# LayerNorm sums of a two-layer decoder step: the last tile is added on VectorE and the totals go to TensorE as high and low fp32r parts

## The reference, cut to what matters

```python
D_MODEL, D_FF, DEPTH, SEQ, DEC_BATCH, DEC_SEQ = 1024, 2816, 2, 256, 8, 4

def _layernorm(x, g, b):
    mu = jnp.mean(xf, axis=-1, keepdims=True)
    var = jnp.mean(jnp.square(xf - mu), axis=-1, keepdims=True)
    y = (xf - mu) * lax.rsqrt(var + LN_EPS) * g + b

def _layer(x, k_mem, v_mem, conv_buf, lru_buf, h0, W):
    x = _layernorm(DN_ALPHA * x + 0.5 * _swiglu(x, ffn1_wg, ffn1_wu, ffn1_wd), ln1_g, ln1_b)
    m, new_conv, new_lru_buf, h_last = _mixer(x, ...)
    x = _layernorm(DN_ALPHA * x + m, ln2_g, ln2_b)
    x = _layernorm(DN_ALPHA * x + 0.5 * _swiglu(x, ffn2_wg, ffn2_wu, ffn2_wd), ln3_g, ln3_b)
    return x, new_conv, new_lru_buf, h_last
```

## Time and profile before

| | us |
|---|---|
| median of 3 runs | 1402.26 |
| lowest and highest run | 1397.68 and 1403.48 |
| the profiled execution, its own time | 1398.62 |
| the profiled execution, its span | 1396.7 |

### The profile page before, as it was taken

How to read it: one execution, slowest core, us unless ns; L and a number is a source line. 1 busy time by engine, 2 the same in 40 slices (tenths; PEclk the granted TensorE clock), 3 DMA queues, 4 the chain that set the end, 5 groups by cost and what they waited for, 6 DMA issues and landing times.

```text
span 1396.7 us, 25445 instructions
## 1 busy us (share of the span) xinstructions
PE 1376.4 (99%) x10566; PEld 1357.0 (97%) x10566; DVE 898.2 (64%) x1180; ACT 666.4 (48%) x896; POOL 35.1 (3%) x68
## 2 busy tenths in 40 slices
PE   8999999999999999999999999999999999999996
PEld 8999999999899999999999999999998999999996
DVE  5555568586865885554685555686887568655444
ACT  5444446445444664444474444463544456544433
POOL 0100000000110000000000000000001000000000
PEclk9999999999999999999999999999999999999998
DMA  6644444654746454444445544445465453554441
GB/s 237 206 178 158 151 168 157 232 176 159 257 176 207 164 182 157 174 155 162 167 166 179 180 155 149 168 164 197 166 236 199 158 195 134 181 178 154 172 166 57
DMA packets 39997, 243.60 MB, mean 174 GB/s; under 512 B 4576, under 2 KB 4592, under 8 KB 16368
## 3 DMA queue, kind: packets, MB, share of 16 engines
q1 hardware_dynamic: 33264, 219.00, 44.9%
q0 software_dynamic: 5936, 22.01, 4.4%
q10 hardware_dynamic: 720, 1.47, 0.3%
HBM read 238.97 MB, written 3.50 MB: 174 GB/s over the span
## 4 chain that ended last, share of the span: by engine, by line
PE 92%; DVE 4%; DMA 1%; ACT 1%; issue 1%; DVEq 0%; ACTq 0%
PE ps L438 29%; PE ps L437 29%; PE ps L439 29%; DVE wlo L1021 1%; DMA raw<-in_w_in 1%; PE ps L525 1%; PE ps L629 1%; PE ps L652 0%; PE ps L597 0%; ACT whi L725 0%; PE ps L636 0%; DMA raw<-in_ffn_wg 0%; PE ps L469 0%; PE ps L470 0%; PE ps L474 0%
## 5 line engine op out<-in xcount | busy, mean ns | idle before, releaser
L1021 DVE TENSOR_TENSOR wlo<-raw,whi 128x1024 fp32r<-128x1024 f32 (+1 forms) x450 | 511.2, 1142 | 320.1 <-ACT whi L725 315.6
L725 ACT CAST whi<-raw 128x1024 fp32r<-128x1024 f32 (+1 forms) x446 | 437.9, 987 | 507.7 <-PE ps L439 394.7
L437 PE MATMUL ps<-xh,whi 128*128 128x288 f32 (+1 forms) x2144 | 635.1, 296 | 1.6 <-DVE xl L1220 1.1
L438 PE MATMUL ps<-xl,whi 128*128 128x288 f32 (+1 forms) x2144 | 631.3, 294 | 0.0
L439 PE MATMUL ps<-xh,wlo 128*128 128x288 f32 (+1 forms) x2144 | 630.6, 294 | 0.0
L437 PEld LDWEIGHTS ps<-xh,whi 128*128 128x128 f32 x2144 | 404.6, 189 | 3.6 <-DVE xl L1220 1.6
L438 PEld LDWEIGHTS ps<-xl,whi 128*128 128x128 f32 x2144 | 406.5, 190 | 0.8
L439 PEld LDWEIGHTS ps<-xh,wlo 128*128 128x128 f32 x2144 | 405.6, 189 | 0.0
L437 PE MATMUL ps<-hh,whi 128*128 128x288 f32 (+1 forms) x1088 | 322.2, 296 | 0.0
L439 PE MATMUL ps<-hh,wlo 128*128 128x288 f32 (+1 forms) x1088 | 319.4, 294 | 0.0
L438 PE MATMUL ps<-hl,whi 128*128 128x288 f32 (+1 forms) x1088 | 319.4, 294 | 0.0
(11 more groups left out here) (186 smaller groups left out, 745.7 us busy)
## 6 DMA issues: line engine op xcount, KB each, us to landing
raw<-in_w_in SPq DMA_DIRECT2D x48, 1024.0 KB, 4.9
raw<-in_ffn_wg SPq DMA_DIRECT2D x43, 1024.0 KB, 4.8
raw<-in_ffn_wu SPq DMA_DIRECT2D x43, 1024.0 KB, 4.8
raw<-in_ffn_wd SPq DMA_DIRECT2D x32, 1024.0 KB, 4.9
raw<-in_ffn_wd SPq DMA_DIRECT2D x16, 768.0 KB, 4.2
pool<-in_cache_k POOLq DMA_DIRECT2D x16, 512.0 KB, 4.3
pool<-in_cache_v POOLq DMA_DIRECT2D x16, 512.0 KB, 4.5
raw<-in_w_o SPq DMA_DIRECT2D x8, 1024.0 KB, 5.0
```

Of the source, the lines that this page charges most:

```text
L437: mm(out, wh, mh, start=start, stop=False)
L438: mm(out, wh, ml, start=False, stop=False)
L725: s_.copy(whi[:, s, k0:k1, :], raw[:, s, k0:k1, :]).then_inc(hi_ready, 1)
L1021: return v.tensor_tensor(out, full, high.bitcast(F32), sub)
```

## The change

For norms 0 to 4 the two early float32 matmuls of `sums` are left out of `last_block`, and so are the two of the eighth tile. VectorE adds the eighth tile and its square to `sums` as well (two additions of 128x288). ScalarE casts both totals to fp32r high parts, into the tiles `hh[20]` and `hh[21]` that the stage no longer needs, and VectorE makes the low parts in `hl[20]` and `hl[21]`. Four fp32r matmuls, `stat_parts(0)` behind the second tile of the early block and `stat_parts(1)` behind its third, multiply them with `ones`. Norm 5 keeps the old form. The sums are the same in number and position; two semaphores `stat_hi` and `stat_lo` are new, and `summed` now counts ten steps for each norm.

```diff
--- before.py
+++ after.py
@@ -148,7 +148,8 @@
         kt = sb("kt", [P, AH, M])
         vt = sb("vt", [P, MT, AH * HEAD])
         ident = sb("ident", [P, P])
-        ones = sb("ones", [P, P])
+        ones_r = sb("ones", [P, P], F32R)
+        ones = ones_r[:, :].bitcast(F32)
         bd = sb("bd", [P, 2, KB, P])
         pts = sb("pts", [P, L, NPR])
         sts = sb("sts", [P, L, KB, NST])
@@ -248,6 +249,7 @@
         ffn_tanh, ffn_hi, h_ready = sem("ffn_tanh"), sem("ffn_hi"), sem("h_ready")
 
         summed, sq_ready, stats_psum = sem("summed"), sem("sq_ready"), sem("stats_psum")
+        stat_hi, stat_lo = sem("stat_hi"), sem("stat_lo")
         mean_ready, msq_ready, var_ready, rstd_ready = sem("mean_ready"), sem("msq_ready"), sem("var_ready"), sem("rstd_ready")
         centred, normed, y_last = sem("centred"), sem("normed"), sem("y_last")
         fill_out = sem("fill_out")
@@ -381,7 +383,7 @@
             pool_e.wait_ge(consts, 1)
             g.affine_select(out=ident[:, :], in_=ident[:, :], compare_op=ALU.not_equal, fill=1.0, base=0,
                             pattern=[[-1, P]], channel_multiplier=1).then_inc(consts, 1)
-            g.memset(ones[:, :], 1.0 / D).then_inc(consts, 1)
+            g.memset(ones, 1.0 / D).then_inc(consts, 1)
             for i, c in enumerate((4.0, 2.0, 4.0)):
                 g.memset(eps[:, i:i + 1], EPS * c * c).then_inc(consts, 1)
             g.memset(junk[:, :], 1.0).then_inc(consts, 1)
@@ -476,7 +478,7 @@
                     if k in (KD // 2 - 1, KD - 1):
                         last.then_inc(pe_half, 1)
 
-            def early_block(n, q, blocks, behind_first):
+            def early_block(n, q, blocks, behind):
 
                 s = n % 2
                 pe.wait_ge(drained, n - blocks)
@@ -488,8 +490,8 @@
                             c = slice(t * P, (t + 1) * P)
                             last = products(ps[:, t, 0:T + 2], whi[:, s, k, c], wlo[:, s, k, c],
                                             xh_wide[:, k, 0:T + 2], xl_wide[:, k, 0:T + 2], k == 0, k == KD - 1)
-                        if k == 0:
-                            behind_first()
+                        if k in behind:
+                            behind[k]()
                     last.then_inc(pe_half, 1)
 
             def first_of_x(n, q):
@@ -522,16 +524,23 @@
                 q, s, fills = 3 * l + ln, n % 2, gap(3 * l + ln)
 
                 def stat(kind, tile, first=False, last=False):
-                    return mm(ps[:, 4 + kind, 0:T], ones[:, :], tile, start=first, stop=last)
+                    return mm(ps[:, 4 + kind, 0:T], ones, tile, start=first, stop=last)
+
+                def stat_parts(kind):
+                    pe.wait_ge(stat_hi, 2 * q + kind + 1)
+                    pe.wait_ge(stat_lo, 2 * q + kind + 1)
+                    mm(ps[:, 4 + kind, 0:T], ones_r[:, :], hh[:, KF - 2 + kind, :], start=True, stop=False)
+                    mm(ps[:, 4 + kind, 0:T], ones_r[:, :], hl[:, KF - 2 + kind, :],
+                       start=False, stop=True).then_inc(stats_psum, 1)
 
                 cut = halves(K)[0][1]
                 for t in range(2):
                     for k in range(K):
                         if t == 0 and k in (0, cut):
                             pe.wait_ge(lo_ready, 2 * n + (k > 0) + 1)
-                        if t == 1 and k == K - 1:
+                        if t == 1 and k == K - 1 and q == 3 * L - 1:
                             for kind in range(2):
-                                pe.wait_ge(summed, 8 * q + 7 + kind)
+                                pe.wait_ge(summed, 10 * q + 7 + kind)
                                 stat(kind, sums[:, kind, 0, :], first=True)
                         mh, ml = operand(k)
                         c = slice(t * P, (t + 1) * P)
@@ -551,7 +560,7 @@
                 if q == 3 * L - 1:
                     stats()
                     return
-                early_block(n + 1, q, blocks, stats)
+                early_block(n + 1, q, blocks, {1: lambda: stat_parts(0), 2: lambda: stat_parts(1)})
                 if fills:
                     pe.wait_ge(mem_lo, 2 * (splits.index(q) + 1))
                     fill(*fills[0])
@@ -836,6 +845,9 @@
                     act.wait_ge(drained, n + 1)
                     s_.activation(sq[:, 1, :], y[:, KD - 1, :], ACT.Square).then_inc(sq_ready, 1)
                     if more:
+                        for kind in range(2):
+                            act.wait_ge(summed, 10 * q + 9 + kind)
+                            s_.copy(hh[:, KF - 2 + kind, :], sums[:, kind, 0, :]).then_inc(stat_hi, 1)
                         gained(l, ln, KD - 1)
                     act.wait_ge(stats_psum, 2 * q + 1)
                     s_.activation(msq[:, :], ps[:, 4, 0:T], ACT.Square).then_inc(msq_ready, 1)
@@ -1138,7 +1150,7 @@
                                            ps[:, bank:bank + 2, 0:T], mult, add).then_inc(drained, blocks)
 
                 def sum_pair(n, j, q):
-                    done, squared = 8 * q, 5 * q
+                    done, squared = 10 * q, 5 * q
                     if j == 0:
                         return
                     dve.wait_ge(drained, n + 1)
@@ -1181,7 +1193,7 @@
                             dve.wait_ge(y_tail, q + 1)
                         else:
                             dve.wait_ge(sq_ready, 5 * q + 4)
-                        dve.wait_ge(summed, 8 * q + 5 + kind)
+                        dve.wait_ge(summed, 10 * q + 5 + kind)
                         v.tensor_tensor(sums[:, kind, 0], sums[:, kind, 0], tile, add).then_inc(summed, 1)
                     if ln == 1:
                         gained_pair(PAIRS_D - 2, l, ln)
@@ -1193,8 +1205,17 @@
                     v.scalar_tensor_tensor(y[:, KD - 1, :], x[:, KD - 1, :], scale, ps[:, bank + 1, 0:T],
                                            mult, add).then_inc(drained, blocks)
                     if more:
+                        for kind, tile in enumerate((y[:, KD - 1, :], sq[:, 1, :])):
+                            if kind == 0:
+                                dve.wait_ge(drained, n + 1)
+                            else:
+                                dve.wait_ge(sq_ready, 5 * q + 5)
+                            dve.wait_ge(summed, 10 * q + 7 + kind)
+                            v.tensor_tensor(sums[:, kind, 0], sums[:, kind, 0], tile, add).then_inc(summed, 1)
+                        for kind in range(2):
+                            dve.wait_ge(stat_hi, 2 * q + kind + 1)
+                            rest(hl[:, KF - 2 + kind, :], sums[:, kind, 0, :], hh[:, KF - 2 + kind, :]).then_inc(stat_lo, 1)
                         lo(n + 2, 0)
-                        dve.wait_ge(drained, n + 1)
                         gained(l, ln, KD - 1)
                     dve.wait_ge(stats_psum, 2 * q + 2)
                     dve.wait_ge(msq_ready, q + 1)
```

## The result

| | before | after |
|---|---|---|
| median of 10 runs, us | 1402.02 | 1408.31 |
| lowest and highest, us | 1397.08 and 1406.68 | 1402.94 and 1410.64 |
| ratio to before, 95% interval | | 1.0039 (1.0024 to 1.0054) |
| the profiled execution's own time, us | 1398.62 | 1402.94 |
| its span, us | 1396.7 | 1401.0 |

What follows compares the result with a forecast made beforehand. The prediction took TensorE's matmul stream, busy 99%, and waits opening in it at the norms as the bound. It summed 3 x 0.37 + 1.35 + 2.0 = +4.5 us onto 1402.3, giving 1406.8 us, range 1399 to 1412.

Steps and rivals of the forecast that it cites:

- The shift of the chain: VectorE's work behind the eighth tile, variance and tiles of x included, moves 2.0 us later; bounds 1.5 and 2.4.
- The early block at norms 0, 2, 3: TensorE waits 0.64 plus 0.11 us before the first new matmuls and leaves the block 0.75 us ahead of before.
- Behind it: After the early block at norms 0, 2, 3, a later half split makes TensorE 0.37 us later at the fifth tile.
- The margin of 0.77: Slack in us between the second half split of the first block on x and TensorE's fifth tile, after hand-over.
- Tile eight at norms 1 and 4 is held by VectorE: Tile eight comes no earlier there; TensorE waits 1.90 plus 0.11 us, leaving norm 1's early block 0.2 us later.
- Norm 1, +1.35: Behind norm 1's early block the split comes 2.0 us later, so 1.35 us are lost at the fifth tile.
- a rival at 6%: Clock falls to half rate behind new waits at norms 1 and 4: 6.4 us more, +10.9 in all, 1413.2; 6%.
- the sign that I had named for a loss of over 7 us: A granted clock under 1 behind norms 1 or 4 would mean a loss over 7 us.
- Norm 4, +2.0: No filler stands at norm 4 and TensorE already waits for x, so the whole 2.0 us goes through.
- The work just leaves the bounding engine: Rival: TensorE's stream shrinks and nothing new waits, -7.7 us, 1394.6; 7%.
- The filler covers norms 0 to 3: Rival: a split or cast comes earlier than counted, hiding the shift there; -0.1 us, 1402.2; 11%.
- No margin at all: Rival: stretched weight supply behind each norm lets every shift through in full; +7.1 us, 1409.4; 10%.

Runs made afterwards that it cites:

- dead_work: Kernel before plus the added VectorE and ScalarE work with results unread, TensorE's stats untouched; timed ratio 1.0037 to the kernel before.
- lo_earlier: Changed kernel with the VectorE weight split that the fifth tile waits for moved behind tile 4 of x, not 5; ratio 1.0021 to the kernel before.
- pe_alone: Kernel before with the four float32 matmuls of norms 0 to 4 made fp32r on constants, sums left out; timed ratio 0.9961.
- stats_later: Changed kernel with the new matmul pairs one tile later at norms 0, 2, 3, two at norms 1, 4; ratio 1.0019 to the kernel before.
- norms_14: The change at norms 1 and 4 only, norms 0, 2 and 3 as in the kernel before; timed ratio 1.0016 to the kernel before.
- parts_of_seven: Kernel before; at norms 0, 2, 3 only seven tiles' sums split, ahead of tile eight, which keeps float32 matmuls; timed ratio 0.9983.

## Why the prediction was right, and where it was off

- **The size.** Forecast +4.5 us within no change, 1406.8; measured +5.5 (3.4 to 7.6), median 1408.3, inside the range of 1399 to 1412 and within 0.5%. The sum of the norms is +5.3, and 0.8 of it is not in the forecast's terms (norm 1, below).
- **The shift of the chain,** 2.0 us, between 1.5 and 2.4: 1.93 at norm 0 (3.87 against 1.94), and 1.90 to 1.93 at the five norms of dead_work. The estimate from the Trainium skill's "Perfetto Trace Analysis", section "Optimizing Scalar/DVE Operations", of 0.36 us for an instruction, 1.44 for four, falls short here. The page calls its overhead a busy time, about doubled in the profiled latency; the estimate with the doubled one is 0.42, still short. The instructions start 0.48 apart where each waits for another, as 217.50, 217.98 and 218.46 show.
- **The early block at norms 0, 2, 3.** A wait of 0.64 and 0.11 for the start, 0.75; the rows give 0.71 (0.84 from start to start, less a step). TensorE leaves the block 0.66 us ahead where I had 0.75.
- **Behind it.** +0.37 forecast for each, +0.31, +0.32 and +0.40 measured, with waits of 0.70 to 0.73 at the fifth tile. The margin of 0.77 was the right number for that row, but I took it for the only one: lo_earlier shows that once it is gone, the last tile of x and the next block's weights bind in its place.
- **Tile eight at norms 1 and 4 is held by VectorE.** Right: the wait there is 1.96 us (2.09 less a step), forecast 2.01, and pe_alone shows the same from the other side.
- **Norm 1, +1.35: off.** It is +2.13 in the profile. Its own terms held, since stats_later, where no clock falls in the early block, gives +1.31. Missing was the clock, which I had as a rival at 6% for a loss of 6.4 us on top. The step that failed is the one by which a wait of 1.2 us that left the clock up spoke for one of 1.9. It does fall behind 1.8 us of idle time, in most profiles; the mean clock of the ten timed runs is 0.994, against 0.996 for before in the later comparisons, though such a mean covers the mixer stages too. So the sign that I had named for a loss of over 7 us came, and that loss did not. TensorE left this block 1.78 us later than before, and not 0.2; in lo_earlier, with the same wait and no fall, it was 0.30. But the price of the rival was sized wrong too: 0.8 and 0.2 us and not 6.4. The clock was down for 3.5 us and not for the whole block, and of the 1.5 us by which the block grew only the 0.83 came through by which the variance was late; for the rest TensorE would have waited for x or weights anyway.
- **Norm 4, +2.0:** +2.16, and +1.92 where the early block kept its clock. That is the shift of the variance, nothing more, as forecast.
- **The rivals.** "The work just leaves the bounding engine" fails, and with it, at this place, the rule of the Trainium skill's "Perfetto Trace Analysis", section "Identifying the Most-Contended Engine": TensorE was at 99% and VectorE at 64%, and work taken from the one and given to the other made the kernel slower. "The filler covers norms 0 to 3" fails on the margin. "No margin at all" is nearly what dead_work measures, +7.1, because there TensorE's start is not earlier.
- **What was not foreseen:** how far the mixer stages scatter by themselves, -2 to +5 us from one execution to another, with a fall of the clock in the long ones. Whether transfers set those waits was not tried. This scatter is as large as the effect, so that the near hit of the median (1408.3 to 1406.8) says less for the forecast than the norms do.

## What to carry to other kernels

Read an engine's load at the place of the change, not over the span: an engine at 64% can be the bound for the 8 to 13 us between a stage's last matmul and the first on the next stage's x (7.8 at norm 4, 13.2 at norm 0 before), and there each of its instructions costs its full length once the margin (0.77 us here) is used up. Work that is moved onto it belongs ahead of the point where it waits for its input; two casts and two subtractions of that kind cost nothing ahead of tile eight. A margin is read over all that the queue must still deliver, and over the queue that feeds it. And where a dense matmul stream gets a new wait, count with the clock behind it, but price it by the results that the slowed matmuls hold up.

## What the runs showed of the hardware

- The granted clock fell from 1.00 to 0.50 for about 3.5 us behind a wait with 1.80 us of idle time (norms 1 and 4 of the changed kernel and of norms_14, norm 4 of lo_earlier); behind an equal wait at norm 1 of lo_earlier it did not, nor behind one of 1.72 in dead_work. Steps of 288 columns went from 0.13 to 0.24 us.
- A float32 matmul of 288 columns took 0.48 us of the stream (two records of 0.24), an fp32r one 0.13.
- On VectorE an addition or subtraction of 128x288 that waits for ScalarE or for the one before started 0.48 us behind it (217.50, 217.98, 218.46). The two subtractions of parts_of_seven, which find their data ready, started 0.37 apart (0.83 for both, 0.46 for one).
